# Expert scores of the last 32 tokens moved from TensorE's matrix to gathered rows of expert_u on VectorE, with three edits of the end

## The reference, cut to what matters

```python
q = (xt @ w_pq).reshape(n_tok, 8, 2, 128)            # queries
scores = einsum('thcd,hckd->thck', q, sub_keys)       # 128 keys in each half
... top 16 of each half, top 16 of their 256 sums -> expert_idx, gate = softmax
u = take(expert_u, idx)                               # 16384 experts x 2048
act = gelu(einsum('thkd,td->thk', u, xb))             # 8 heads x 16 experts a token
v = take(expert_v, idx)
out = einsum('thk,thkd->td', gate * act, v)
```

## Time and profile before

| | |
|---|---|
| three runs | 1876.03, 1876.7, 1881.94 us (median 1876.7) |
| profiled execution | 1876.2 us, of which the span is 1874.4 us |
| PE busy | 1850.5 us (99%) |
| PE weight load | 1572.4 us (84%) |
| DVE | 1280.2 us (68%) |
| ACT | 1018.8 us (54%) |
| POOL | 1055.0 us (56%) |
| mean DMA rate | 254 GB/s |
| mean granted clock of PE | 0.996 |
| chain of waits | PE 96%, DVE 2%, DMA 1% |

### The profile page before, as it was taken

How to read it: one execution, slowest core, us unless ns; L and a number is a source line. 1 busy time by engine, 2 the same in 40 slices (tenths; PEclk the granted TensorE clock), 3 DMA queues, 4 the chain that set the end, 5 groups by cost and what they waited for, 6 DMA issues and landing times.

```text
span 1874.4 us, 30301 instructions
## 1 busy us (share of the span) xinstructions
PE 1850.5 (99%) x9326; PEld 1572.4 (84%) x9326; DVE 1280.2 (68%) x1886; ACT 1018.8 (54%) x1842; POOL 1055.0 (56%) x769
## 2 busy tenths in 40 slices
PE   9999999999999999999999999999999999999996
PEld 7888888888888888888888888887888888888885
DVE  4555676768565454555555557966898888888887
ACT  4455555545566565555555555555555555555553
POOL 0000231200488989788888887726888666665423
PEclk9999999999999999999999999999999999999998
DMA  7777776664655666788998888977999999999993
GB/s 246 236 240 224 230 239 204 184 204 160 217 170 181 194 186 203 200 192 196 246 230 195 194 192 273 294 232 259 360 390 359 391 338 358 395 375 370 378 341 91
DMA packets 202730, 476.42 MB, mean 254 GB/s; under 512 B 63504, under 2 KB 65744, under 8 KB 201840
## 3 DMA queue, kind: packets, MB, share of 16 engines
q1 hardware_dynamic: 131824, 391.56, 62.0%
q0 software_dynamic: 52416, 80.02, 15.8%
q10 hardware_dynamic: 18432, 4.20, 1.1%
HBM read 453.41 MB, written 21.07 MB: 253 GB/s over the span
## 4 chain that ended last, share of the span: by engine, by line
PE 96%; DVE 2%; DMA 1%; ACT 0%; POOL 0%; issue 0%; SPq 0%; ACTq 0%; DVEq 0%
PE ps L750 25%; PE ps L503 14%; PE ps L505 14%; PE ps L504 14%; PE ps L756 13%; PE ps L790 6%; PE ps L791 6%; PE ps L720 0%; DMA x_nat<-in_x 0%; PE ps L493 0%; DMA act_dram<-halves 0%; DVE stats L1779 0%; PE ps L554 0%; DVE ps L1776 0%; DVE y_out L1801 0%; DVE act_both L1263 0%
## 5 line engine op out<-in xcount | busy, mean ns | idle before, releaser
L750 PE MATMUL ps<-act_both,split_hi 128*128 128x512 f32 x2048 | 513.3, 393 | 0.0
L1059 ACT ACTIVATE split_hi<-raw 128x512 fp32r<-128x512 f32 x512 | 308.0, 625 | 292.2 <-PE ps L756 289.9
L750 PEld LDWEIGHTS ps<-act_both,split_hi 128*128 128x128 f32 x2048 | 368.6, 189 | 65.6
L1509 DVE TENSOR_TENSOR split_lo<-raw,split_hi 128x512 fp32r<-128x512 f32 x368 | 284.0, 788 | 201.7 <-ACT split_hi L1059 197.0
L1179 ACT ACTIVATE v_hi<-v_tile 128x1024 fp32r<-128x1024 f32 x248 | 263.2, 1062 | 254.4 <-PE ps L791 247.0
L1729 DVE TENSOR_TENSOR v_lo<-v_tile,v_hi 128x1024 fp32r<-128x1024 f32 x248 | 308.1, 1265 | 79.1 <-ACT v_hi L1179 78.9
L1250 DVE TENSOR_TENSOR split_lo<-raw,split_hi 128x512 fp32r<-128x512 f32 x304 | 232.5, 771 | 162.1 <-ACT split_hi L846 161.1
L846 ACT ACTIVATE split_hi<-raw 128x512 fp32r<-128x512 f32 x344 | 216.4, 631 | 226.7 <-PE ps L505 224.4
L1927 POOL DMA_INDIRECT gate_dram<-pick_n,places x192 | 300.3, 1564 | 59.4 <-issue 59.4
L1975 POOL DMA_INDIRECT rows<-in_expert_v,picked x128 | 208.4, 1629 | 189.3 <-DVE row_sum L1741 116.7
L756 PEld LDWEIGHTS ps<-act_both,split_lo 128*128 128x128 f32 x2048 | 279.6, 190 | 19.9
(11 more groups left out here) (206 smaller groups left out, 2131.8 us busy)
## 6 DMA issues: line engine op xcount, KB each, us to landing
raw<-in_expert_u SPq DMA_DIRECT2D x256, 512.0 KB
v_tile<-in_expert_v SPq DMA_DIRECT2D x256, 512.0 KB, 7.0
raw<-in_w_in SPq DMA_DIRECT2D x112, 512.0 KB
raw<-in_w_out SPq DMA_DIRECT2D x32, 512.0 KB
raw<-in_w_pq SPq DMA_DIRECT2D x32, 512.0 KB
gate_dram<-zeros SPq DMA_DIRECT2D x24, 512.0 KB, 5.7
gates<-gate_dram POOLq DMA_DIRECT2D x64, 192.0 KB, 4.6
act_dram<-halves ACTq DMA_DIRECT2D x128, 32.0 KB
```

Source lines behind the costliest of these rows:

```text
L750: return nc.tensor.matmul(ps[:, bank, :], split_hi[:, q % SPLITS, i * P:(i + 1) * P], act_both[:, k, :, :].rearrange("p a t -> p (a t)"), ...
L1059: nc.scalar.activation(split_hi[:, q % SPLITS, :], raw[:, q // 2, q % 2, :], ACT.Copy).then_inc(hi_ready, 1)
L1509: vec.tensor_tensor(split_lo[:, q % SPLITS, :], raw[:, q // 2 % RAWS, q % 2, :], split_hi[:, q % SPLITS, :].bitcast(f32), ALU.subtract).th ...
```

## The change

1. **Scores.** The last 32 tokens (OWN) leave the score stage's matmuls: 2 x 224 columns in the wide ones, 224 in the narrow ones (UT = 224). The scores of their 32 x 128 chosen experts are computed from gathered rows: the 4096 pairs of token and expert are laid out as 32 rounds (DOTS) of 128 partitions. In each, POOL gathers 128 rows of expert_u (8 KB each) into one of two slots, and DVE multiplies them by the tokens' x1 and sums, in two halves of 1024 columns. Dot j stands in DVE's list in pair 22 + j, and POOL's gather j in its list between scatters, one every six from the 25th on.
2. POOL moves `dot_rows` in four more small DMAs; SP and DVE wait for all eight.
3. expert_v is loaded ahead in pairs 55 to 62, after the dots, since their slots lie in its tiles.
4. POOL applies 32 pairs of gates, not 48, before the next stage's rows; the rest are between rows.
5. `weigh` goes from POOL to DVE. The dots' results go through ACT's gelu, are moved by four DMAs of POOL (`move_dots`) and are weighed by DVE before the first row.
6. The last two tiles of weights get buffers of their own (`wlast`) and are split before the slots of 122 and 123 are free.
7. The move of `row_sum`'s upper half is issued by POOL as soon as the last row is added.
8. DVE does the sums of FULL ahead of the norms of PART; one quarter of PART's norm goes to ACT and POOL, the other stands behind FULL's variance.

```diff
+OWN = HB // 2
+UT = DENSE + OWN
+DOT_SLOTS, DOT_AT = 2, 22
+DOTS = OWN * PKEYS // P
-PREFETCH = 30
+PREFETCH = 55
-APPLIED_AHEAD = 48
+APPLIED_AHEAD = 32
...
             with sp.Fori(1, DOT_AT - 1) as i:
                 u_pair(i)
-            sp.wait_ge(picked_in, 64)
+            sp.wait_ge(picked_in, 128)
             sp.wait_ge(topk_done, 2)
+            sp.wait_ge(x1_out, X1_OUT)
+            for g in range(4):
+                sp.dma_start(x1_own[OWN * g:OWN * g + OWN, :], x1_dram[P - OWN:P, PART, :]).then_inc(own_in, 16)
+            with sp.Fori(DOT_AT - 1, PREFETCH) as i:
+                u_pair(i)
+            sp.wait_ge(dot_used, 2 * DOTS)
...
-                    return nc.tensor.matmul(ps[:, bank, :], split_hi[:, q % SPLITS, i * P:(i + 1) * P],
-                                            act_both[:, k, :, :].rearrange("p a t -> p (a t)"), start=k == 0,
-                                            stop=k == KT - 1)
+                    return nc.tensor.matmul(ps[:, bank, 0:2 * UT].rearrange("p (a t) -> p a t", a=2),
+                                            split_hi[:, q % SPLITS, i * P:(i + 1) * P], act_both[:, k, :, 0:UT],
+                                            start=k == 0, stop=k == KT - 1)
...
+            def dot(j, slot, half):
+                cols = slice(half * UNIT, half * UNIT + UNIT)
+                part = u_slots[slot][:, cols]
+                vec.scalar_tensor_tensor(out=part, in0=part, scalar=1.0, in1=x1_own[:, cols], op0=ALU.mult, op1=ALU.mult,
+                                         accum_out=dots[:, half, bass.ds(j, 1)]).then_inc(dot_used, 1)
-            def u_pair(pair, parity):
+            def u_pair(pair, parity, j=None):
                 for k in (2, 3):
                     split_two(pair, parity, k)
+                    if j is not None and k == 2:
+                        dve.wait_ge(u_row_in[parity], pair * 8 - (DOT_AT + parity) * 8 + 16)
+                        dot(j, parity, 0)
                 add_halves(pair, 0, 2 * parity)
                 for k in (4, 5):
                     split_two(pair, parity, k)
+                    if j is not None and k == 4:
+                        dot(j, parity, 1)
...
+                    def load_u_row(j):
+                        if j >= DOT_SLOTS:
+                            pool.wait_ge(dot_used, 2 * (j - DOT_SLOTS) + 2)
+                        eng.indirect_dma_start(u_slots[j % DOT_SLOTS][:, :], None, u_v,
+                                               bass.IndirectOffsetOnAxis(ap=dot_rows[:, j:j + 1], axis=0)
+                                               ).then_inc(u_row_in[j % DOT_SLOTS], 16)
+                    def rows_at(h, b, k):
+                        n = h * sum(per_head) + b * TOPK + k - h * TOPK
+                        j = DOT_SLOTS + (n - 24) // 6
+                        return j if n >= 24 and n % 6 == 0 and j < DOTS else 0
...
+                    for g in range(4):
+                        eng.dma_start(dot_rows[OWN * g:OWN * g + OWN, :],
+                                      places_u[P - OWN:P, 3, DOTS * g:DOTS * g + DOTS]).then_inc(picked_in, 16)
...
+            def weigh_dots():
+                dve.wait_ge(dot_in, 64)
+                for half in range(2):
+                    some = slice(half * HB + OWN, half * HB + HB)
+                    vec.tensor_tensor(picked_w[some, :], dot_act[some, :], picked_gate[some, :], ALU.mult
+                                      ).then_inc(dot_weighed, 1)
...
                     for j in range(2, ROW_SLOTS):
                         load_row(j)
-                    weigh(0)
+                    move_dots()
+                    acts_landed(0)
...
+            act.wait_ge(applied, PAIRS)
+            for i in range(2):
+                nc.scalar.activation(wlast[i][:, HID:HID + HB], wexp[:, NT - 2 + i, P:DENSE], ACT.Copy)
+                nc.scalar.activation(wlast[i][:, HI0:HI0 + DENSE], wexp[:, NT - 2 + i, 0:DENSE], ACT.Copy
+                                     ).then_inc(last_w_hi, 1)
...
             summed(FULL, 0)
             end_shift(PART)
-            for q in range(2):
-                end_norm(PART, q)
             for q in range(1, 4):
                 summed(FULL, q)
             end_var(FULL)
+            end_norm(PART, 0)
             end_shift(FULL)
```

More of the change, by code:

```diff
@@ L132, in layer_kernel @@
         picked_w = at("picked_w", [HB], f32, KEEP + 12288)
-        halves = at("halves", [4, SEQ], f32, KEEP + 9216)
+        halves = at("halves", [4, UT], f32, KEEP + 9216)
+        dot_rows = at("dot_rows", [DOTS], u32, KEEP + 8192)
+        dots = at("dots", [2, DOTS], f32, KEEP + 12800)
+        dot_act = at("dot_act", [HB], f32, KEEP + 13056)
         zeros = at("zeros", [4, SEQ], f32, KEEP + 9216)
         wsplit = at("wsplit", [4, WCOLS], f32r, KEEP + 5120)
+        wlast = [at(f"wlast{i}", [WCOLS], f32r, KEEP + (1024, 12800)[i]) for i in range(2)]
         wexp = at("wexp", [NT, DENSE], f32, W0)
@@ L470, in _ @@
             quarters = out.rearrange("a (b p) (q d) -> (a p) b q d", p=P, d=COLS)
-            for b, q, ready, count in ((PART, 0, y_ready, 1), (PART, 1, y_ready, 2), (PART, 2, y_last, 1),
-                                       (PART, 3, y_last, 2), (FULL, 0, y_ready, 3), (FULL, 1, y_ready, 4),
-                                       (FULL, 3, y_last, 3), (FULL, 2, y_ready, 5)):
+            for b, q, ready, count in ((PART, 2, y_last, 1), (PART, 3, y_last, 2), (PART, 0, y_ready, 1),
+                                       (PART, 1, y_last, 3), (FULL, 0, y_ready, 2), (FULL, 1, y_ready, 3),
+                                       (FULL, 3, y_last, 4), (FULL, 2, y_ready, 4)):
                 sp.wait_ge(ready, count)
@@ L1709, in _ @@
             dve.wait_ge(x1_out, X1_OUT)
-            dve.wait_ge(picked_in, 64)
-            with dve.Fori(PAIRS_A // 2, PAIRS // 2 - 1) as i:
+            dve.wait_ge(picked_in, 128)
+            with dve.Fori(PAIRS_A // 2, DOT_AT // 2) as i:
+                for s in range(2):
+                    u_pair(i * 2 + s, s)
+            dve.wait_ge(own_in, 64)
+            with dve.Fori(DOT_AT // 2, (DOT_AT + DOTS) // 2) as i:
+                for s in range(2):
+                    u_pair(i * 2 + s, s, i * 2 + (s - DOT_AT))
+            dve.wait_ge(dot_used, 2 * DOTS)
+            vec.tensor_tensor(dots[:, 0, :], dots[:, 0, :], dots[:, 1, :], ALU.add).then_inc(dot_summed, 1)
+            with dve.Fori((DOT_AT + DOTS) // 2, PAIRS // 2 - 1) as i:
                 for s in range(2):
@@ L1730, in split_v, with weigh @@
                                   v_hi[:, unit % UNITS, :].bitcast(f32), ALU.subtract).then_inc(v_lo_ready, 1)
+            def weigh_dots():
[4 more added lines that the diff above has]
+                                      ).then_inc(dot_weighed, 1)
+            def weigh(k):
+                part = slice(k * W_GROUP, (k + 1) * W_GROUP)
+                dve.wait_ge(act_in[k % 2], 16 * W_GROUP * (k // 2 + 1))
+                for half in range(2):
+                    some = slice(half * HB, half * HB + OWN)
+                    vec.tensor_tensor(picked_w[some, part], picked_act[some, part], picked_gate[some, part], ALU.mult
+                                      ).then_inc(weight_ready, 1)
             def add_row(j):
+                if j % W_GROUP == 0:
+                    weigh(j // W_GROUP)
                 dve.wait_ge(row_in[j % ROW_SLOTS], 32 * (j // ROW_SLOTS + 1))
-                dve.wait_ge(weight_ready, j // W_GROUP + 1)
+                dve.wait_ge(weight_ready, 2 * (j // W_GROUP) + 2)
+                dve.wait_ge(dot_weighed, 2)
                 row, weight = rows[j % ROW_SLOTS][:, :], picked_w[:, j:j + 1]
@@ L1943, in _ @@
                     pool.wait_ge(zeroed, 16 * ZEROS)
+                    for j in range(DOT_SLOTS):
+                        load_u_row(j)
                     for h in range(PH):
@@ L1950, in _ @@
                             scatter(h, b)
+                    for j in range(DOT_SLOTS + (PH * sum(per_head) - 24) // 6, DOTS):
+                        load_u_row(j)
                     for b in range(TB):
@@ L2027, in _ @@
                     end_affine(PART, 3, 1)
-            end_affine(FULL, 3, 2)
+            end_affine(PART, 1, 2)
+            end_affine(FULL, 3, 3)
 def constant_tables():
```

84 lines of the change are left out of this document (53 added, 31 removed).

## The result

The kernel after the change takes **1943.3 us**, median of 4 runs (1939.4 to 1948.0), against 1876.6 before: ratio 1.035, 95% interval [1.032, 1.038]. Forecast were 1886 us and a range up to 1908. The profiled execution took 1942.6 us, its span is 1940.8.

| stretch | forecast | measured |
|---|---|---|
| to the end of the score stage, the first product of the value stage (1271.7 before, 1326.1 after) | +8.3 | +54.4 |
| from there to the first product of the held tiles | +7.5 | +8.9 |
| from there to VectorE's last operation | -5.6 | -2.7 |
| from there to the end of the span | 0 | +5.8 |

What follows compares the result with a forecast made beforehand. PE set the pace at 11.17 us a pair, with POOL's list, so far waited for by nobody, becoming what DVE waits for. 8.3 + 7.5 - 5.6 = +10.2 on 1876.2 gave 1886 us, range 1864 to 1908.

Steps and rivals of the forecast that it cites:

- The value start: Start of the value stage: POOL's late moves of the dots' values make PE wait, 7.5 us later (bounds 0 and 9).
- Scatters have not got faster: 11.24 us.: Dots' pairs: six scatters between gathers keep 11.24 us; with a gather of 1.75, a dot every 13.0 us.
- Rival B: Dots' pairs: DVE's dots hold POOL back, or 8 KB rows cost more; +32 us: 1918, or +60; chance 0.12.
- The last dots: End of the dots: gather 31 starts at 1167.2, lands 8.5 us later, then 3.1 us; pair 54 starts at 1178.8.
- Pairs 54 to 63: Score stage's end beside gates: 6.6 pairs of 10.2 and 3.4 of 9.85, 101 us (bounds 98.5 and 112).
- Pairs 0 to 17: Score stage's start: PE waits for POOL's low parts, 10.3 us a pair, 15.7 us gained; pair 18 at 741.7.
- the picks: Around pair 18: DVE's chain ends later and four more POOL DMAs follow, a PE stall of some 4.5 us.
- The end: Held tiles and last norms: own weight buffers 5.1 us, sums ahead of norms 0.5; together 5.6 us less.
- narrower products: Score stage's matmuls: fewer columns, taken alone, make a pair 9.85 us, 84.5 us less over 64 pairs.

Runs made afterwards that it cites:

- e1: The changed kernel without gathers of u rows and without dots, so the narrower matmuls alone: 1845.5 us, ratio 0.9819 to the kernel before.
- e4: The changed kernel with a gather after every four scatters, not six: 1890.6 us, ratio 1.0061 to the kernel before.
- e6: The changed kernel with the four moves of the dots' GELU values issued before the first row gathers: 1940.4 us, ratio 1.0316 to the kernel before.
- e9: The changed kernel without gathers and dots, with score matmuls back at 512 and 256 columns: 1890.3 us, ratio 1.0062 to the kernel before.
- e5: The changed kernel with 12 instead of 32 pairs of gates applied ahead of the value stage: 1946.2 us, ratio 1.0336 to the kernel before.
- e2: The changed kernel with each dot covering 8 columns in place of 1024: 1912.7 us, ratio 1.0177 to the kernel before.
- e12: The changed kernel with two waits a pair of POOL for its own last low part, in pairs 1 to 17: 1945.4 us, ratio 1.0352 to before.
- e3: The changed kernel with the dots reading x1 from PSUM instead of SBUF: 1927.4 us, ratio 1.0255 to the kernel before.
- e7: The changed kernel with gathers every four scatters, early moves, 12 pairs of gates ahead and later added rows: 1852.4 us, ratio 0.9839 to before.
- e10: The kernel with gathers every four scatters, early moves and late rows, plus x1 in PSUM and 16 pairs of gates ahead: 1847.8 us, ratio 0.9838.
- e8: The kernel before with the end's edits alone, no gathers, dots or narrower products: 1878.3 us, ratio 0.9987 to the kernel before.
- e14: The kernel with gathers every four scatters, x1 in PSUM and 16 pairs of gates, plus one POOL wait a pair in pairs 1 to 17: 1837.2 us.
- e11: The kernel before with ten more semaphores that nothing uses: ratio 1.0001 to the kernel before.
- e13: The kernel before with expert_u given twice, in rows and in tiles, the rows never read: 1885.6 us, ratio 1.0050 to the kernel before.

## Why the prediction was wrong, by its own steps

**What was right.** The sign, the mechanism and its place. POOL's list, which nobody waited for, became one that DVE waits for; POOL set the pace of pairs 24 to 53, DVE's idle time before the dots ends with the rows' landing, and PE follows (e1, e4). The value start came out at +8.9 for +7.5, with the moves as its cause (e6):

```profile
1363.43 0.47 DVE L1788 TENSOR_TENSOR picked_w<-dot_act,picked_gate 32x64 f32<-32x64 f32 x2 [9.13 <-DMA dot_act<-dots]
```

```profile
1366.84 0.80 PE L522 MATMUL ps<-v_hi,wsplit 128*128 128x512 f32 x1 [5.83 <-DVE v_lo L1780]
```

It came with a slow stretch of PE, at a granted clock of 0.50, the lower of its two levels:

```profile
1366.84:1371.27 4.43, 4.43 (x10) 3.48 (x11) 4.43 (x4) 0.00 (x0) 3.80 (x4) 0.50 0.58 147
```

**The failing step: "Scatters have not got faster: 11.24 us."** They got slower. The 1.873 us of the earlier trace rows was a property of the pace, not of the operation. At 11.17 us a pair the scatters stood at the same six places of every pair, where they took 1.54 to 1.65 us, and at any other pace measured the mean is 1.65 to 1.80 us (e1 at 10.09 us a pair, with no dot or gather, 1.71; e9, back at 11.17, 1.563). Six cost 11.98 us, not 11.24. With the gather's 1.69 (forecast 1.75) rows come every 13.66 us in place of 13.0. Gather 31 started at 1188.9, not 1167.2. Of these **21.7 us** the scatters make 23.8, and a wait of 2.65 us for the slot of dot 29 comes on top; the first gather was 2.7 us early and the gathers 1.9 us cheaper. The whole score stage ended 46.3 us later than forecast (1326.1 for 1279.8). I took the mean spacing of the kernel before as the price and held one value for it in the range, where the gather had two. Rival B had such a price, but for the gathers and through the dots; here it fell on the scatters, 0.74 us a pair, and e1 shows it without any dot.

**The last dots, 12.9 us.** From the start of gather 31 to PE's start of pair 54 I had 11.6 us, and the trace 24.5 (to 1213.35). I let the last row meet an idle DVE. But the gates began at 1198, and dot 31 stood behind dot 30 (1193.43 and 1206.07 us); its half took 2.53 us beside POOL's gates, in place of 1.22.

**Pairs 54 to 63, 11.7 us.** I had 101 us and it took 112.7, and all but a few tenths of the difference lie in pairs 54 to 57. "10.2 us a pair, as DVE was busy 10.05" took DVE's time for a fixed load. Over 61 us beside the gates DVE was busy without a break:

```profile
1200.00:1261.00 61.00, 51.45 (x289) 45.84 (x288) 61.00 (x51) 28.34 (x64) 50.42 (x63) 0.94 0.84 277
```

Its low parts took 1.56 us there, against 0.69 between 900 and 1100. e5 gives 8.2 us of this and of pair 53 back with fewer gates. Gates alone do not do it (e1 and e2 run 10.09 us beside all 32): it is gates on a DVE that is already behind with full dots. PE's own pace, 10.09 instead of 9.85, adds less than 1 us here. A narrow matmul took 0.110 us for the forecast 0.106, a wide one 0.205 for 0.202.

**Pairs 0 to 17 and the picks.** POOL had no idle time left, and a pair took 10.15 us, not 10.3, so that PE began pair 18 at 738.4, by the reading that gave 757.4 before, and not at 741.7. The picks cost 5.6 us in pair 18, for 4.5:

```profile
738.44 2.01 PE L769 MATMUL ps<-act_both,split_hi 128*128 128x448 f32 x9
742.23 1.33 PE L775 MATMUL ps<-act_both,split_lo 128*128 128x224 f32 x8 [1.78 <-DVE split_lo L1535]
```

DVE's operation of 11.54 us stood in the chain, and without it (e12) the pair still loses 5.1. The forecast took a POOL without idle time as harmless to others. That this trace loses no more by it is luck: in the traces of e1, e3 to e7 and e10 each operation of 15.4 to 16.0 us cost PE 4.4 to 9.6 us.

**The end, -2.7 for -5.6.** PE's stall at the held tiles went and the slow stretch with it, as forecast; but POOL's early sum of the row halves (5.22 us at 1899.08) stands beside DVE's low parts, whose eight take 14.7 us, before 9.2, and PE now waits for these twice (1.15 and 1.06 us). e8 confirms the size; no run moves the sum alone.

**Behind the last operation, +5.8.** Not in the forecast. SP's waits show what it is: first for the last store, then for PE's sequencer, long after PE's last matmul at 1922.1.

```profile
SPq L110 <- PEq L110: 5.5, 1, 5.5
SPq L110 <- DMA out_y<-y_out: 2.6, 1, 2.6
```

Before it was 0.4 us. It is 5.5 us in after, e1 to e4, e9 and e12, 4.8 in e6, and 0.2 to 0.9 in e5, e7, e10 and e14, with the same work for PE in all but e9; not the end's edits (e8), the semaphores (e11) or the second input (e13). What delays the sequencer stays open.

**Where the gain of narrower products went.** At PE's measured pace it is 64 x 1.08 = 69 us, not 84.5. e1 shows 33 us of it in the time (1878.9 to 1845.5); in its trace the rest lies in two operations of 15.4 and 15.9 us, which cost PE 13 us, in 7 us at the picks, in 15 us of the value stage, most of it one stall of 11.7 us, and in the 5.8 us at the end. A gather every 6 scatters takes all of the 33 us and 65 more. With one every 4, x1 in PSUM, moves first, rows late and one gap a pair the kernel is 41 us faster than before (e14).

## What to carry to other kernels

Before taking a duration from a trace into a new schedule, ask whether it depends on the phase between two engines. If n of them with their issue make exactly one period of the loop (6 x 1.868 = 11.2), the trace shows n phases only, and at another period there will be others (five, with two of them long, at 10.1); the range must hold their values. In a list in program order, count the distance between the items that somebody waits for, not the list's total; moving the same gathers from every 6 to every 4 scatters was worth 53 us. And when a change takes an engine's last idle time away, look for who shares a port with it: with one gap of 0.16 us a pair the best kernel was 10 us faster, and its trace lost an operation of 16 us by it. Two gaps a pair in the changed kernel, whose trace had no such operation, gained nothing (e12).

## What the runs showed of the hardware

- One to three operations of VectorE with two inputs in SBUF (128x128 and 128x256) took 11.5 to 16.0 us in each trace, in place of 0.4 to 1.6, while GpSimd ran its elementwise operations without a gap; gaps of 0.16 us ended that (e12, e14). Which operation is caught varies from run to run (0.88 or 15.98 us for the same line).
- GpSimd's gathers of half a row took 0.94 to 3.3 us, and scatters average 1.56 us at 11.17 us a pair and 1.65 to 1.80 at others; at 10.09 us a pair without gathers, five to a pair, two of the five take 1.95 and 2.00 us and the others 1.54 (e1).
- A pair of 32 wide and 32 narrow matmuls took 10.09 us at 448 and 224 columns, 11.17 at 512 and 256: 12.5% fewer columns gave 9.7% less time.
